# Gate projections of a two-layer trunk: seven block products for the latent tiles instead of eight, and the first modulation in other PSUM banks

## What is computed

```python
proj = jnp.einsum('bsd,dn->bsn', h, lp['w_in'])
(a_q, a_k, a_v, b_q, b_k, b_v, c_z, c_xbc, c_dt, d_q, d_k, d_v, gate) = split_proj(proj)
...
up = jnp.einsum('bsnw,nwd->bsnd', branches, lp['w_br'])
g = jax.nn.sigmoid(gate.reshape(Bz, S, N_BRANCH, D_MODEL))
out = jnp.einsum('bsd,de->bse', jnp.sum(g * up, axis=2), lp['w_out'])
...
hid = jax.nn.silu(jnp.einsum('becd,edf->becf', xs, w1)) * jnp.einsum('becd,edf->becf', xs, w3)
yo = jnp.einsum('becf,efd->becd', hid, w2) * gval[..., None].astype(x.dtype)
```

## Time and profile before

| | us |
|---|---|
| median of 3 runs | 1917.54 (1916.52 to 1919.07) |
| profiled execution | 1917.25 |
| its span | 1915.5 |
| experts of layer 0, first matmul | 510.60 |
| first products of layer 1's branch C | 981.30 |

### The profile page before, as it was taken

The page is one execution under the profiler, slowest core; times in us unless marked ns, Lnnn a source line. Parts: engine busy times, 40 slices in busy tenths (PEclk is TensorE's granted clock), DMA queues, the critical chain, the costliest instruction groups (busy, mean ns, idle before and its releaser), DMA issues.

```text
span 1915.5 us, 19402 instructions
## 1 busy us (share of the span) xinstructions
PE 1817.3 (95%) x7696; PEld 801.8 (42%) x7696; DVE 484.4 (25%) x1227; ACT 366.4 (19%) x930; POOL 49.4 (3%) x91
## 2 busy tenths in 40 slices
PE   6999999999899998998989999999998999989987
PEld 3564444444434332432355544444444343324322
DVE  1252322454411010110022542225633011101101
ACT  2232222231501000100023332222233010001000
POOL 2100300000000000000000000000000000000000
PEclk9999999999999999999999999999999999999999
DMA  9364420325699999999965461320348999999997
GB/s 380 114 248 183 132 89 21 110 88 232 243 383 431 429 431 430 429 431 429 426 246 203 159 261 50 110 82 29 132 192 330 379 413 425 431 430 428 431 430 307
DMA packets 66685, 532.90 MB, mean 278 GB/s; under 512 B 6880, under 2 KB 7008, under 8 KB 42816
## 3 DMA queue, kind: packets, MB, share of 16 engines
q1 hardware_dynamic: 63472, 527.59, 67.8%
q0 software_dynamic: 3152, 4.47, 0.7%
HBM read 529.16 MB, written 2.88 MB: 278 GB/s over the span
## 4 chain that ended last, share of the span: by engine, by line
PE 76%; DMA 18%; DVE 3%; ACT 1%; issue 1%; SPq 0%; ACTq 0%; DVEq 0%
PE bank L688 68%; DMA ring<-in_w_e 16%; PE bank_pair L688 4%; PE bank L697 4%; DMA ring<-in_w_ada 1%; DMA ring<-in_w_in 1%; DVE x L2443 0%; DVE scr L2157 0%; ACT xn L1711 0%; DVE scr L2330 0%; ACT scr L1787 0%; DVE scr L2329 0%; ACT scr L1789 0%; DVE xn L2159 0%; ACT L1453 0%
## 5 line engine op out<-in xcount | busy, mean ns | idle before, releaser
L688 PE MATMUL bank<-ring,hT 128*128 128x512 f32 (+2 forms) x1376 | 575.4, 570 | 4.7 <-DMA ring<-in_w_in 2.5
L688 PE MATMUL bank<-ring,scr 128*64 128x512 f32 (+1 forms) x2152 | 524.5, 600 | 46.4 <-DMA ring<-in_w_e 35.5
L688 PEld LDWEIGHTS bank<-ring,hT 128*128 128x128 f32 x1376 | 256.6, 192 | 263.7 <-issue 250.3
L688 PE MATMUL bank<-scr 128*64 128x512 f32 (+4 forms) x1612 | 338.1, 545 | 1.1 <-DVE scr L2432 1.1
L688 PEld LDWEIGHTS bank<-ring,scr 128*64 128x64 f32 (+1 forms) x2152 | 173.7, 142 | 365.7 <-issue 295.0
L688 PEld LDWEIGHTS bank<-scr 128*64 128x64 f32 (+3 forms) x1612 | 116.1, 148 | 188.4 <-issue 184.5
L2428 DVE TENSOR_TENSOR scr<-scr,bank 128x512 f32<-128x512 f32 x32 | 22.0, 688 | 459.4 <-PE bank L688 459.4
L1799 ACT ACTIVATE scr<-bank 128x512 f32<-128x512 f32 x32 | 19.1, 597 | 459.1 <-PE bank L688 459.1
L697 PEld LDWEIGHTS bank<-cst,scr 128*128 128x128 f32 (+1 forms) x538 | 63.6, 158 | 94.3 <-issue 52.6
L688 PE MATMUL bank_pair<-scr 32*128 32x512 f32 (+6 forms) x352 | 102.1, 501 | 0.0
L697 PE MATMUL bank<-cst,scr 128*128 128x128 f32 (+1 forms) x538 | 90.0, 288 | 10.0 <-DVE scr L2240 3.3
(11 more groups left out here) (264 smaller groups left out, 1069.6 us busy)
## 6 DMA issues: line engine op xcount, KB each, us to landing
ring<-in_w_e SPq DMA_DIRECT2D x122, 2048.0 KB, 18.9
scr<-in_w_e SPq DMA_DIRECT2D x64, 2048.0 KB, 19.0
ring<-in_w_ada SPq DMA_DIRECT2D x24, 2048.0 KB, 9.6
ring<-in_w_in SPq DMA_DIRECT2D x20, 2048.0 KB, 9.0
ring<-in_w_out SPq DMA_DIRECT2D x4, 2048.0 KB, 8.9
ring<-in_w_in SPq DMA_DIRECT2D x4, 1552.0 KB, 13.2
ring<-in_w_in SPq DMA_DIRECT2D x4, 1536.0 KB, 10.6
ring<-in_w_br SPq DMA_DIRECT2D x4, 1024.0 KB, 5.0
```

Source lines behind the costliest of these rows:

```text
L688: ins = pe.matmul(out, lhsT, rhs, start=start, stop=stop, **kw)
```

## The change

Each gate's latent part (256 tokens x 1024 inputs x 1024 columns) is cut into 2 x 2 blocks and computed with seven block products P1 to P7 of four matmuls each. Four sums of weight blocks (128 x 2048 each) are made by POOL for every gate; two of them lie in a ring slot that carries no load for that time (`("sums", i)` in `ORDER`), two overwrite raw weights once these have been used. Four sums of token blocks are made once a layer by POOL, in the upper half of slot 3 and in place in hT. DVE adds the products up in the gate's SBUF tile (seven operations), ACT then applies tanh there. The prompt tile is still computed with 16 matmuls, ahead of the products. Gate 0's P2, P6, P5, P7 go to banks 6, 7, 4, 5.

```diff
-ORDER = (("ada", 0), ("ada", 1), ("C", 0), ("D", 0), ("ada", 3), ("AB", 0), ("ada", 4), ("ada", 5), ("gate", 0), ("ada", 2),
-         ("gate", 1), ("lift", 0), ("lift", 1), ("gate", 2), ("lift", 2), ("gate", 3), ("lift", 3), ("out", 0))
+ORDER = (("ada", 0), ("ada", 1), ("C", 0), ("D", 0), ("ada", 3), ("AB", 0), ("ada", 4), ("ada", 5), ("ada", 2), ("gate", 0),
+         ("sums", 0), ("lift", 0), ("gate", 1), ("sums", 1), ("gate", 2), ("sums", 2), ("lift", 1), ("gate", 3), ("sums", 3),
+         ("lift", 2), ("lift", 3), ("out", 0))
+HOME = {("ada", 0): (2, 3), ("ada", 1): (0, 1), ("C", 0): (2, 3), ("D", 0): (0, 1), ("ada", 3): (2, 3), ("AB", 0): (2, 3),
+        ("ada", 4): (0, 1), ("ada", 5): (0, 1), ("ada", 2): (0, 1), ("gate", 0): (0, 1), ("sums", 0): (2,), ("lift", 0): (3,),
+        ("gate", 1): (2, 0), ("sums", 1): (1,), ("gate", 2): (1, 2), ("sums", 2): (0,), ("lift", 1): (3,), ("gate", 3): (0, 1),
+        ("sums", 3): (2,), ("lift", 2): (3,), ("lift", 3): (2,), ("out", 0): (0, 1)}
+UNITS = ("a0", "a1", "b0", "b1", "P1", "P2", "P6", "P5", "P7", "P3", None, "P4")
```

On SP the loads wait for the sums; on POOL the sums stand ahead of transfers:

```diff
+                after_sums = {AT_GATE[1]: 4, AT_GATE[2]: 8, AT_GATE[3]: 12, AT_LIFT[3]: 16}
+                    if j in after_sums:
+                        sp.wait_ge(sums_ready, li * 16 + after_sums[j])
...
+                    pool.wait_ge(freed[SLOT[j]], li * PER[SLOT[j]] + TURN[j])
+                    landed(AT_GATE[i])
+                    pool.tensor_tensor(sum_block(i, 0), block(i, 0, 1), block(i, 0, 0), ALU.subtract).then_inc(sums_ready, 1)
...
+                    pool.tensor_tensor(sum_block(i, 1), block(i, 1, 1), sum_block(i, 0), ALU.subtract).then_inc(sums_ready, 1)
+                def last_sums(i):
+                    pool.wait_ge(used_raw, now(used_raw, 2 * i + 1))
+                    pool.tensor_tensor(block(i, 0, 1), block(i, 1, 1), block(i, 0, 1), ALU.subtract).then_inc(sums_ready, 1)
+                    pool.wait_ge(used_raw, now(used_raw, 2 * i + 2))
...
+                    pool.tensor_tensor(block(i, 1, 0), block(i, 1, 0), sum_block(i, 1), ALU.subtract).then_inc(sums_ready, 1)
+                first_sums(0)
...
+                pool.tensor_tensor(tsums[:, 0], a21, a22, ALU.add).then_inc(row_sums, 1)
...
+                last_sums(0)
                 pool.wait_ge(ab_ready, now(ab_ready, 1))
...
+                first_sums(1)
+                last_sums(1)
+                if more_layers:
+                    pool.wait_ge(mod1, now(mod1, 2))
+                    columns(li + 1)
+                    quarters(li + 1)
+                for i in (2, 3):
+                    first_sums(i)
+                    last_sums(i)
```

On PE `rows(5)` moves ahead of ab_unit(3) and `rows(2)` ahead of ab_unit(4). Gate 0 is then: four prompt halves (a0, a1, b0, b1), dT, cdT, ckT, P1, P2, P6, P5, P7, `qkT`, P3, P4. Gates 1 and 2 do two entries of `UNITS` in each of their six attention steps, so the sixth has only P4, behind `pair_weights`. Gate 3 does one in each of steps 1 to 11, and `lift(2,0)` moves into step 12:

```diff
-                    if 1 <= n <= NIT:
-                        gate(3, (n - 1) // 2, (n - 1) % 2)
-                for t in range(2):
-                    lift(2, t)
+                    if 1 <= n < NIT:
+                        unit(3, n - 1 if n < NIT - 1 else NIT - 1)
+                    elif n == NIT:
+                        lift(2, 0)
+                lift(2, 1)
                 turned(3)
...
-                pe.wait_ge(merged, now(merged, 18))
                 for k in range(KD):
+                    if k % 4 == 0:
+                        pe.wait_ge(merged, now(merged, 17 + k // 4))
```

```diff
-                if li:
-                    pe.wait_ge(x_final, li * NT)
-                    busy(1)
-                bs = [bank(("row", 0, h)) for h in range(2)]
+                bs = [banks[6], banks[7]] if li else [banks[2], banks[3]]
...
                 columns(0)
+                if li:
+                    early_turns()
```

In the experts a zero matmul at the end of each expert goes (slot 5 is then released by yp_ready), and the two parts of the scatter take other tiles (`LATE_SUMS`, `EARLY_SUMS`):

```diff
-                    owed.append(freed[s])
-                    mm(banks[0][:, 0:8], c_("zero"), c_("zero")[:, 0:8], start=False, stop=False, skip_group_check=True)
```

More of the change, by code:

```diff
@@ L47 @@
 AT_C, AT_D, AT_AB, AT_OUT = (AT[name, 0] for name in ("C", "D", "AB", "out"))
-AT_GATE, AT_LIFT = ([AT[name, i] for i in range(4)] for name in ("gate", "lift"))
+AT_GATE, AT_LIFT, AT_SUMS = ([AT[name, i] for i in range(4)] for name in ("gate", "lift", "sums"))
+UNITS = ("a0", "a1", "b0", "b1", "P1", "P2", "P6", "P5", "P7", "P3", None, "P4")
+SUMMED = {(1, 0): 1, (2, 1): 2, (1, 1): 3, (2, 0): 4}
 SLOTS_E = 6
@@ L101, in big_results @@
     out = []
-    out += [(("row", 0, h), "act") for h in range(2)] + [(("col", 0, j), "dve") for j in range(2)]
+    out += [(("col", 0, j), "dve") for j in range(2)]
     out += [(("hT", k), "dve" if k % 2 else "act") for k in range(4, KD)]
@@ L767, in _ @@
                     for c in range(2):
[L768 to L776, removed]
+                        if v and c and li == 0:
+                            early_turns()
                         need(j + c)
@@ L936, in _ @@
                 columns(3)
+                for h in range(2):
+                    rows(5, h)
                 ab_unit(3)
@@ L962, in gate0, with prompt_half @@
-                def gate0(s):
-                    for part in range(2):
-                        gate(0, s, part)
-                gate0(0)
-                gate0(1)
-                for h in range(2):
-                    rows(2, h)
+                gate_bank = [None, None]
+                def prompt_half(i, part, h):
+                    if h == 0:
+                        need(AT_GATE[i] + part)
+                    if part == 0:
+                        gate_bank[h] = bank(("g", i, 0, h))
+                    for k in range(4):
+                        sig = None
+                        if k == 3:
+                            sig = big if part else used_raw if h else None
+                        mm(gate_bank[h][:, :], hT[:, 4 * part + k, 0:P], block(i, part, h)[:, k, :], start=part == 0 and k == 0,
+                           stop=part == 1 and k == 3, signal=sig)
@@ L970, in _, with unit @@
+                def unit(i, n):
+                    u = UNITS[n]
+                    if u is None:
+                        return
+                    if u[0] == "P":
+                        product(i, u)
+                    else:
+                        prompt_half(i, "ab".index(u[0]), int(u[1]))
+                for n in range(4):
+                    unit(0, n)
                 pe.wait_ge(d_ready, now(d_ready, 1))
@@ L980, in _ @@
                 turn(b[:, P:2 * P], ch("bk"), signal=big)
-                for s in range(2, 5):
-                    gate0(s)
+                product(0, "P1")
+                for n, p in enumerate(("P2", "P6", "P5", "P7")):
+                    product(0, p, banks[(6, 7, 4, 5)[n]], early_prod)
                 pe.wait_ge(ab_ready, now(ab_ready, 1))
@@ L1489, in _ @@
                 for h in range(2):
-                    rows(0, h)
+                    act.wait_ge(mod_rows, now(mod_rows, h + 1))
+                    A(rsb[0][:, h * HALF:(h + 1) * HALF], banks[(6 if li else 2) + h][:, :], ACT.Copy).then_inc(mod_taken, 1)
                 act.wait_ge(mod1, now(mod1, 1))
```

259 lines of the change are left out of this document (194 added, 65 removed).

## The result

The changed kernel takes 1952.2 us (median of 4 runs, 1947.7 to 1954.9) against 1917.5 for the kernel before: a ratio of 1.018, with a 95% interval of 1.0167 to 1.0193. The forecast was 1900.5, faster, in a range of 1887 to 1922. It was wrong in sign, and the time lies 30 us above the range's end. The profiled execution took 1954.22 us for a span of 1952.4.

What follows compares the result with a forecast made beforehand. PE, 95% busy, was taken to bound the kernel, except where DMA is full (548 to 980 us). Layers -7.4 each (-14.8), modulation -0.6, experts -1.6: -17.0 from 1917.25, plus 0.3 for the median, gave 1900.5 us; range 1887 to 1922.

Steps and rivals of the forecast that it cites:

- The sums, "PE waits for none": POOL's weight and token sums in all gates: ready before PE wants them, so no PE wait and no cost.
- the bounds: Time of one POOL sum of 2048 columns: from 1.85 us (one stream) to 5.5 us (three), 5.5 taken.
- The rival that took turns: POOL sums and DVE operations on two SBUF inputs exclude each other, deciding in gate 0: 12 us a layer, 1925; chance 0.2.
- Gate 0, +0.6: Gate 0 to first scores, each layer: late start and head_norm chain eat the saving, scores at 222.1, +0.6 us not -3.5.
- The moved rows, 2.3 us (0 to 3.2): rows(5) and rows(2) moved ahead of gate 0: PE waits 2.3 us for ada 2's weights, ends 0 and 3.2.
- Gates 1 and 2, -3.5 each: Attention steps of gates 1 and 2: 4.8 us of slack left, so each gate keeps its full saving of 3.5 us.
- Gate 3 and the tail, -2.7: Tail behind gate 3, each layer: lift(2,0) fills gate 3, PE waits 3.9 us, mT's transposes start earlier; net -2.7 us.
- The clock, +1.7 a layer: PE's clock after idle time: one dip a layer costing 1.7 us, ends 0 and 3.4.
- Modulation, -0.6: Layer 1, ada 0 and 1 before branch C: path some 7 us shorter, but C waits for w_in; 0.6 us gained.
- Experts, -1.6: Experts of both layers: the zero matmul (0.39 us) goes, counting until DMA is full; -1.6 us in all.
- Products, -28: All gates: four fewer matmuls each save 3.5 us a gate, 14 a layer, 28 in all, if PE waits for nothing new.

Runs made afterwards that it cites:

- Small sums: Changed kernel, each POOL weight and token sum cut to one column, waits and signals kept, output lacking the sums: 1905.35 us in one run.
- the hold by itself: Whole computation left out; eleven DVE operation forms timed alone and beside one POOL sum (4.49 us), copy (1.89 us) or fill (1.80 us) of 2048 columns.
- the sums in pieces: Changed kernel with each POOL weight sum cut into four back-to-back operations of 512 columns: 1931.57 us in one run.
- the last part alone: Kernel before with only layer 1's modulation in banks 6 and 7, scatter order, no zero matmul, slot 5 issued by yo_psum: 1915.12 us, ratio 0.9991.
- the sums in the gaps: Changed kernel, sums on DVE where it waits, gate 3's halved, rows(2) one ab_unit later, ACT's third square and root before prompt tanhs: 1894.27 us, ratio 0.9871.

## Why the prediction was wrong, step by step

**The sums, "PE waits for none": the step that failed.** The sum of the forecast has them at nothing, because it asked only whether POOL's results come in time for PE. They do: PE waits for POOL nowhere, and a sum took 4.51 us, inside the bounds. The Trainium skill's price (GPSIMD Engine Reference, section 3.1), 4497 ns, agrees. What was not priced is what a sum does to DVE while it runs: DVE's operations on SBUF stand still, and PE waits for DVE and for ACT behind it. Small sums show what that costs: 46.9 us.

**The rival that took turns** was the right mechanism with 0.2 of the chance and 1925 us; its price was too small three times. It counted only operations with two SBUF inputs; the measurement of the hold by itself shows `tensor_scalar` and copies held too, on two columns as on 512. The Trainium skill's section that it quoted (SBUF — State Buffer, Who interferes with whom) goes on to say that copies and `tensor_scalar` can enter DVE's 2-port modes and so contend; the trace agrees (4.45 us for 0.17). It counted one place, gate 0, and gave "the rest of the kernel" enough slack beside a sum; but a chain of small operations can be held again at each link. Against small sums, the first scores to `lift(0)` take 54.0 us instead of 50.0, and gate 3's steps 65.8 instead of 59.4 (375.08 to 440.92, 354.67 to 414.08). And it left out the clock after PE's waits. Its point of decision, scan outputs after 187, was right: they end at 197.62. Its evidence against, "no row here shows it", was no evidence, since POOL read nothing in the kernel before, as the prediction says itself.

**Gate 0, +0.6:** first scores forecast at 222.1, measured 241.26; with small sums, 226.96. Of that difference of 4.9, 4.3 us lie ahead of gate 0.

**The moved rows, 2.3 us (0 to 3.2):** 3.48 us, just over the end. The pair of ada 2 was issued at 145.6 and 147.5, and its second load landed 12.1 us after its own issue, at 159.6, where 11.1 were assumed; the profile names no releaser, but PE starts at 159.63. Missed with it: the 32 records behind the wait take 5.34 us instead of 3.64, 1.7 more. Branch C at the start of the kernel took 12.29 us for records that took 10.60, at a granted clock of 0.86 there instead of 1.00. That is not the change's doing: with the sums in pieces, whose start is the same program, they took 10.60, and in the last part alone 12.29: it differs from execution to execution. So gate 0 starts at 182.70 and not at 178.0, and 1.7 us of that are chance.

**Gates 1 and 2, -3.5 each:** gate 1, whose three first sums run into the first attention steps, gives +1.1 (54.03 from 52.96), with PE waiting 2.30 us for a held `tensor_scalar`; gate 2 gives -3.8 (68.14 from 71.92), as forecast.

**Gate 3 and the tail, -2.7:** the tail gives -3.5 (21.58 from 25.04), with PE's wait ahead of `turned(3)` 3.48 us where 3.9 were forecast. What was not forecast is the steps before it: +2.0 up to the first weights and +4.8 in gate 3's steps, the place of the holds again. `tensor_scalar` on 128x2 there took 1.00 us in the mean of 24, against 0.17:

```profile
L2386 DVE TENSOR_SCALAR st<-st 128x2 f32<-128x2 f32 x24 | 24.0, 1001 | 0.8
```

**The clock, +1.7 a layer:** one dip was forecast, and the trace has more, each behind a wait of PE. In layer 0 the records of `rows(2)` lost 1.7 us, and the transposes of `qkT` 1.8.

**Modulation, -0.6:** right that the shorter path does not count while DMA is full. But branch C is not released by w_in: after the last scatter PE now waits for the weights of ada (DMA share 1.03 from 980 to 1000 us), and C for ACT, which writes the modulated h (hT) behind them:

```profile
990.83 1.92 PE L758 MATMUL bank<-ring,csw 128*32 128x512 f32 x16 [3.20 <-DMA ring<-in_w_ada]
995.95 3.60 PE L758 MATMUL bank<-ring,csw 128*32 128x512 f32 x16 [3.19 <-DMA ring<-in_w_ada]
...
1004.47 10.60 PE L758 MATMUL bank<-ring,hT 128*128 128x256 f32 x48 [0.96 <-ACT hT L1567]
```

It cost 1.0 us instead of giving 0.6 (last scatter to C: 23.9, from 22.9); in the last part alone, where C does wait for w_in, 0.3.

**Experts, -1.6:** layer 0's take 1.0 us more up to the last scatter (448.8 from 447.8), layer 1's 4.0 less (454.9 from 458.9), 3.0 less in all. The same experts took 446.1 us in layer 0 with the last part alone and 448.5 with the sums in the gaps, so the 1.0 can't be told from the spread; layer 1 gave 3.9 in the first and 4.0 in the second. Why only layer 1 gains is open.

**Products, -28:** no run measures them by themselves. PE has the 64 records less that they account for. Gate 2, in which PE does not wait, gives 3.8 us for its 3.5, and once the holds and the wait at `rows(2)` are gone the kernel is 23 us faster than before.

## What to carry to other kernels

Before work is moved to GpSimd, look at what VectorE does at that time: each `tensor_scalar`, copy or two-input operation on SBUF that meets a GpSimd operation may stand still to its end, however small it is, and a chain of them pays again at each link. Price a "free" engine by what it shares with the engine on the critical chain, not by whether its own result is in time; a rule that speaks against the change deserves more than a rival's chance when the trace of before cannot show the case. Here VectorE did the sums itself in half the time, and the gain came once they stood where it waited anyway.

## What the hardware showed that was not expected

A `tensor_scalar` of 128x2, 0.17 us alone, takes 4.45 us beside a GpSimd sum and 1.66 beside a fill that reads nothing, while a two-input operation passes beside the fill (0.69 us). A reciprocal on the same two columns and a reduction from SBUF pass beside everything (0.17 and 0.69 us). Between two GpSimd operations standing back to back a held VectorE operation gets its turn: with pieces of 512 columns the 128x2 operation in gate 1's first step took 0.50 us instead of 3.75, and the kernel regained 20.6.
